# First modulation quarter summed by k-tile, with two weight units loaded and split in parts

## Chip, cores, metric

One core of one Trainium2 chip. The metric is device time in microseconds (us) of one execution, taken as the median of several runs. TensorE (PE) multiplies, VectorE (DVE), ScalarE (ACT) and GpSimd (POOL) work on elements, SyncE (SP) issues most DMAs.

## What is computed

One layer of a transformer block on 512 tokens of width 1024, all in float32. What matters here is its beginning:

```python
mod = jax.nn.silu(c) @ ada_w[layer] + ada_b[layer]            # c: [1, 1024], ada_w: [1024, 6144]
shift1, scale1, gate1, shift2, scale2, gate2 = jnp.split(mod[:, None, :], 6, axis=-1)
h = rmsnorm(x, norm1_w[layer]) * (1 + scale1) + shift1        # [512, 1024]
gq, gk, gv, gr, g_lr, aq, ak, av, merge_a, merge_b = jnp.split(h @ w_in[layer], split_at, axis=-1)
```

Gated linear attention, dilated attention, the merging and a convolutional feed-forward layer follow; the change doesn't touch them.

## The kernel before

The width of 1024 is cut in 8 k-tiles of 128. To keep float32 accuracy with a fast matrix format, each operand of a product is split into a high part (ScalarE converts) and a low part (VectorE subtracts the high part), and three products are made: high by high, low by high, high by low. Weights come in units of 1 MB (`raw`, two slots), which ScalarE turns into `w_hi` and VectorE into `w_lo`. `hi_done` counts units with a high part, `raw_used` units with a low part; the second also frees the slot of `raw` for the DMA that waits for it in `load(q)`.

The first three units are the value weights: unit 0 (`v`, 256 columns of all 8 k-tiles), units 1 and 2 (`vw`, 512 columns of k-tiles 0 to 3 and 4 to 7). They are multiplied while the normalised input is still being made, quarter by quarter; quarter j is k-tiles 2j and 2j + 1. For each quarter:

- The modulation. `ada_w`'s columns for shift and scale of the two k-tiles land in two halves of 1 MB (`load_first(j)`, line 437; half 0 are rows of k 0 to 3, half 1 rows of k 4 to 7). VectorE multiplies each of 8 rows of 128 x 512 by a column of `c_silu` and adds them up in place (`ada_sums(j, half)`, lines 1111 and 1114; quarter 1 leaves one row to TensorE). TensorE sums over the partitions with four products against `ones` (`shift_scale(j)`, line 1732). VectorE adds the bias and makes the gain (`shift_and_gain(j)`, lines 1124 and 1127).
- The input. TensorE transposes a tile of tokens (`normed_tile(k)`, line 1716) into one of four banks, ScalarE copies it out (`normed_out(k)`, line 714, which counts `xn_sb`), makes the high part of the modulated tile once the gain is there (`high(k)`, line 684) and then the tile itself (`modulated(k)`, line 689); VectorE makes the low part (`lower(k)`, line 1137).
- The products. `quarter_hi(j)` is `first_hi` of two k-tiles (unit 0, line 1990) and then `wide_hi` of two (units 1 and 2, line 2020), high input against high and low weights; `quarter_lo(j)` is `first_lo` (line 1998) and `wide_lo` (line 2025), low input against high weights. `wide_hi(0)` writes the four banks that the transposes use, so it waits for `xn_sb` 5 to 8.

Each engine runs its instructions in the order in which the code lists them, and waits at the head for semaphores. Before the change TensorE's list is: six transposed tiles, `shift_scale(0)`, two tiles, `quarter_hi(0)`, `shift_scale(1)`, `quarter_lo(0)`, `quarter_hi(1)`, `shift_scale(2)` and so on. VectorE's: `ada_sums(0, 0)`, `ada_sums(0, 1)`, `shift_and_gain(0)`, `split_lo(0)`, `split_lo(1)`, `ada_sums(1, 0)`, `ada_sums(1, 1)`, `lower(0)`, `lower(1)`, `shift_and_gain(1)`, ... ScalarE's: four `normed_out`, `split_hi(0)`, `high(0)`, `high(1)`, `split_hi(1)`, four `normed_out`, `modulated(0)`, `modulated(1)`, `high(2)`, ... SP's: `load_first(0)`, `load(0)`, `load(1)`, `load_first(1)`, `load_first(2)`, `load(2)`, `load_first(3)`, `load(3)`, then the spill of `xn`.

Of the kernel before, what the change touches and what calls it, by code (L numbers as in the profile page):

```python
# [16 lines left out]
P = 128  # L17
# [146 lines left out]
DIRECT = {1: KT - 1}  # L164
ADA_STEPS = [KT - (j in DIRECT) for j in range(KT // 2)]
SPLIT_K = 5


def hybrid_block_kernel(nc, x, c, positions, ada_w, ada_b, norm1_w, w_in, gate_w2, gate_b, gla_norm_w,
# [3 lines left out]
    with ctx:  # L173
# [132 lines left out]
        spilled, x_back = sem("spilled"), [sem(f"x_back{i}") for i in range(2)]  # L306
        ada_step, ident_in = sem("ada_step"), sem("ident_in")
        mod1_ps, mod_done, gain_done = sem("mod1_ps"), sem("mod_done"), sem("gain_done")
        sq_done, sum_done, ssq_ps, ln_done, rstd_done = (sem(n) for n in (
# [52 lines left out]
        def normed(k):  # L362

            return n_first[:, k, :] if k < LATE else cs[:, k - LATE, :]

        def last_tile(n):
# [55 lines left out]
        def _(sp):  # L422
# [61 lines left out]
            def shuffle(j):  # L484
# [5 lines left out]
                for half in range(2):  # L490
                    for a in range(4):
                        sp.dma_start(qk[32 * half:32 * half + 32, g, a // 2, a % 2, :],  # L492
                                     rope[32 * a:32 * a + 32, j % 2, half, :]).then_inc(qk_in[j % 2], 16)

            load_first(0)
            load(0)
            load(1)
            load_first(1)
# [132 lines left out]
        def _(act):  # L631
# [48 lines left out]
            def high(k):  # L680

                act.wait_ge(gain_done, k // 2 + 1)
                act.wait_ge(xn_sb, k + 1)
                act.activation(h_hi[:, k, :], xn[:, k, :], ACT.Identity, scale=gain[:, 0, k:k + 1],
                               bias=mod[:, k:k + 1]).then_inc(hh_done, 1)
# [25 lines left out]
            def normed_out(k):  # L711

                act.wait_ge(xn_ps, k + 1)
                act.activation(xn[:, k, :], bank[3 + k % 4][:, :], ACT.Copy).then_inc(xn_sb, 1)

            scaled_tokens(0)
            scaled_tokens(1)
            for k in range(4):
                normed_out(k)
            split_hi(0)  # L720
            high(0)
            high(1)
            split_hi(1)
            for k in range(4, KT):
                normed_out(k)
            modulated(0)
            modulated(1)
            for k in (2, 3):
# [366 lines left out]
        def _(dve):  # L1095
# [8 lines left out]
            def ada_sums(j, half):  # L1104
# [4 lines left out]
                for k in range(half * KT // 2, (half + 1) * KT // 2):  # L1109
                    if k == 0:  # L1110
                        dve.tensor_scalar(total, total, c_silu[:, 0:1], None, ALU.mult).then_inc(ada_step, 1)
                    elif k != DIRECT.get(j):
                        dve.wait_ge(ada_step, sum(ADA_STEPS[:j]) + k)
                        dve.scalar_tensor_tensor(total, ada_rows(j, k), c_silu[:, k:k + 1], total,
                                                 ALU.mult, ALU.add).then_inc(ada_step, 1)

            mod_v = mod[:, 0:2 * KT].rearrange("p (s k) -> p s k", s=2)
            bias_v = vecs[:, V_AB:V_AB + 2 * KT].rearrange("p (s k) -> p s k", s=2)

            def shift_and_gain(j):  # L1120
                two = slice(2 * j, 2 * j + 2)
                dve.wait_ge(mod1_ps, j + 1)
                dve.wait_ge(vec_sb, 1)
                dve.tensor_tensor(mod_v[:, :, two], bank[7][:, 4 * j:4 * j + 4].rearrange("p (s k) -> p s k", s=2),
                                  bias_v[:, :, two], ALU.add).then_inc(mod_done, 1)
                dve.wait_ge(mod_done, j + 1)
                dve.scalar_tensor_tensor(gain[:, 0, two], mod_v[:, 1, two], 1.0, vecs[:, V_N1 + 2 * j:V_N1 + 2 * j + 2],
                                         ALU.add, ALU.mult).then_inc(gain_done, 1)

            def lower(k):  # L1130
# [302 lines left out]
            for b in range(1, NB):  # L1433
                sum_squares(b)
            ada_sums(0, 0)
            ada_sums(0, 1)
            shift_and_gain(0)
            split_lo(0)
            split_lo(1)
            ada_sums(1, 0)  # L1440
            ada_sums(1, 1)
            lower(0)
            lower(1)
            shift_and_gain(1)
            ada_sums(2, 0)
# [248 lines left out]
        def _(pe):  # L1694
# [12 lines left out]
            pe.transpose(bank[2][:, 0:ROWS_A], rows_a[:, :], ident[0:ROWS_A, 0:ROWS_A]).then_inc(vec_ps, 1)  # L1707

            def normed_tile(k):

                if k >= 4:
                    pe.wait_ge(xn_sb, k - 3)
                for b in range(NB):
                    if k == 0:
                        pe.wait_ge(xs_done, b + 1)
                    last = pe.transpose(bank[3 + k % 4][:, b * P:(b + 1) * P], x_tok[:, b, k * P:(k + 1) * P], ident)
                last.then_inc(xn_ps, 1)

            def shift_scale(j):

                for rows, moving, first in ((DIRECT.get(j), c_silu, True), (0, ones, False)):
# [9 lines left out]
                    for n in range(4):  # L1731
                        last = pe.matmul(bank[7][:, 4 * j + n:4 * j + n + 1], ada_rows(j, rows)[:, n * P:(n + 1) * P],
                                         moving[:, rows:rows + 1], start=(n == 0 and (first or j not in DIRECT)),
                                         stop=not first, skip_group_check=True)
                last.then_inc(mod1_ps, 1)

            def take(i):
# [244 lines left out]
            def first_hi(k):  # L1982

                if k == 0:
                    pe.wait_ge(raw_used, 1)
                pe.wait_ge(hh_done, k + 1)
                for blk in range(NB):
                    dst = bank[blk // 2][:, blk % 2 * UW:(blk % 2 + 1) * UW]
                    for v in (w_hi, w_lo):
                        pe.matmul(dst, h_hi[:, k, blk * P:(blk + 1) * P], v[:, 0, k * UW:(k + 1) * UW],  # L1990
# [18 lines left out]
            def wide_hi(k):  # L2009

                unit = UNIT[("vw", k // (KT // 2), 0)]
                for part, v in enumerate(wide_weights(k)):
                    if part == 0:
                        pe.wait_ge(hi_done, unit + 1)
# [31 lines left out]

            for k in range(6):
                normed_tile(k)
            shift_scale(0)
            for k in (6, 7):  # L2050
                normed_tile(k)
            quarter_hi(0)
            shift_scale(1)
# [209 lines left out]
```

## Time and profile before

| | |
|---|---|
| median of 3 runs | 927.73 us (926.24 to 928.46) |
| the profiled execution | 928.56 us, span 926.8 us |
| TensorE busy | 899.6 us, 97% of the span |
| TensorE weight loads | 767.6 us, 83% |
| VectorE busy | 493.3 us, 53% |
| ScalarE busy | 369.0 us, 40% |
| GpSimd busy | 36.1 us, 4% |
| chain that ended last | TensorE 88%, SP's queue 3%, ScalarE 3%, VectorE 3%, DMA 2% |

Busy times overlap; an engine that idles while another sets the pace costs nothing. The stretch in question is the first 45 us, in which TensorE still waits for others. "PEclk" is TensorE's granted clock, where 1.00 is 2.4 GHz and 0.50 is 1.2 GHz.

### The profile page before, as it was taken

To read this page: it belongs to the slowest core of one execution; us is meant where nothing else is said; L and a number is where in the kernel's file an instruction comes from. 1 tells how busy PE (TensorE), PEld (TensorE's weight loads), DVE (VectorE), ACT (ScalarE), POOL (GpSimd) and SP (SyncE) were. 2 spreads that over 40 slices of the span, in tenths; PEclk is the share of its full clock that TensorE was granted. 3 is DMA by queue.
4 is the path that set the end of the run, shared out by engine and by line. 5 is a ranking of instruction groups with operands and counts; after the bars stand their busy time and mean duration, and the time that the engine had idled before them with its cause. 6 is when DMAs were issued, how large, how long until landed. Compare 5 with 4: busy or idle time off the path is not lost.

```text
span 926.8 us, 11681 instructions
## 1 busy us (share of the span) xinstructions
PE 899.6 (97%) x4581; PEld 767.6 (83%) x4581; DVE 493.3 (53%) x568; ACT 369.0 (40%) x459; POOL 36.1 (4%) x33
## 2 busy tenths in 40 slices
PE   3999999999999999999999999999999999999996
PEld 3998788989898888887888888888888888888885
DVE  5877875637372737451444667555555555522223
ACT  6442216593533446252223334333333334322235
POOL 0010000000000000000022110000000000000003
PEclk9899999999999999999999999999999999999998
DMA  9965726214351434353233341333333332232202
GB/s 324 347 186 155 195 41 195 65 46 159 114 182 46 160 113 140 133 184 110 71 136 118 112 134 46 92 91 91 91 107 110 99 91 91 105 113 100 91 0 92
DMA packets 117101, 112.91 MB, mean 122 GB/s; under 512 B 7380, under 2 KB 107094, under 8 KB 114631
## 3 DMA queue, kind: packets, MB, share of 16 engines
q1 hardware_dynamic: 116343, 110.21, 38.0%
q10 hardware_dynamic: 720, 2.16, 0.7%
q8 instruction: 27, 0.44, 0.2%
q14 instruction: 11, 0.09, 0.0%
HBM read 104.80 MB, written 4.21 MB: 118 GB/s over the span
## 4 chain that ended last, share of the span: by engine, by line
PE 88%; SPq 3%; ACT 3%; DVE 3%; DMA 2%; issue 1%; DVEq 0%; ACTq 0%
PE bank L1700 25%; PE bank L1702 24%; PE bank L1701 24%; SPq L492 2%; PE bank L2020 1%; DMA raw<-in_w_in_dram 1%; PE bank L2174 1%; PE bank L1921 1%; PE bank L1820 1%; PE bank L1949 1%; DVE w_lo L1154 1%; PE bank L1916 1%; PE bank L2025 1%; PE bank L1815 1%; PE bank L1792 1%
## 5 line engine op out<-in xcount | busy, mean ns | idle before, releaser
L1700 PE MATMUL bank<-h_hi,w_hi 128*128 128x512 f32 x672 | 265.1, 395 | 1.6 <-DVE w_lo L1154 0.8
L1702 PE MATMUL bank<-h_hi,w_lo 128*128 128x512 f32 x672 | 261.7, 389 | 0.0
L1701 PE MATMUL bank<-h_lo,w_hi 128*128 128x512 f32 x672 | 261.6, 389 | 0.0
L1700 PEld LDWEIGHTS bank<-h_hi,w_hi 128*128 128x128 f32 x672 | 126.2, 188 | 28.2 <-issue 2.8
L1702 PEld LDWEIGHTS bank<-h_hi,w_lo 128*128 128x128 f32 x672 | 126.1, 188 | 26.4
L1701 PEld LDWEIGHTS bank<-h_lo,w_hi 128*128 128x128 f32 x672 | 126.3, 188 | 25.3 <-issue 0.2
L1154 DVE TENSOR_TENSOR w_lo<-raw,w_hi 128x2048 fp32r<-128x2048 f32 (+2 forms) x46 | 85.6, 1872 | 86.9 <-ACT w_hi L646 86.9
L1161 DVE TENSOR_TENSOR w_lo<-raw,w_hi 128x2048 fp32r<-128x2048 f32 x31 | 71.1, 2293 | 86.3 <-ACT w_hi L654 86.3
L1654 DVE SCALAR_TENSOR_TENSOR conv<-bank,vecs,conv 128x511 f32<-128x511 f32 x88 | 65.7, 748 | 65.8 <-ACT conv L1046 60.3
L646 ACT ACTIVATE w_hi<-raw 128x2048 fp32r<-128x2048 f32 (+2 forms) x44 | 71.7, 1642 | 50.2 <-DMA raw<-in_w_in_dram 50.1
L654 ACT ACTIVATE w_hi<-raw 128x2048 fp32r<-128x2048 f32 x31 | 59.1, 1906 | 69.3 <-PE bank L1702 69.3
L1046 ACT ACTIVATE conv<-bank,vecs 128x512 f32<-128x512 f32 x44 | 34.2, 779 | 104.7 <-PE bank L1702 104.7
L1700 PE MATMUL bank<-hs_hi,w_hi 128*128 128x512 f32 x176 | 68.6, 390 | 0.0
L1702 PE MATMUL bank<-hs_hi,w_lo 128*128 128x512 f32 x176 | 68.5, 389 | 0.0
L1701 PE MATMUL bank<-hs_lo,w_hi 128*128 128x512 f32 x176 | 68.5, 389 | 0.0
L1700 PEld LDWEIGHTS bank<-hs_hi,w_hi 128*128 128x128 f32 x176 | 33.0, 188 | 6.9
L1702 PEld LDWEIGHTS bank<-hs_hi,w_lo 128*128 128x128 f32 x176 | 33.0, 188 | 6.8
L1701 PEld LDWEIGHTS bank<-hs_lo,w_hi 128*128 128x128 f32 x176 | 33.0, 188 | 6.8
L1700 PE MATMUL bank<-w_hi,h_hi 128*128 128x256 f32 x128 | 37.2, 290 | 0.1
L1701 PE MATMUL bank<-w_lo,h_hi 128*128 128x256 f32 x128 | 36.7, 287 | 0.0
L1702 PE MATMUL bank<-w_hi,h_lo 128*128 128x256 f32 x128 | 36.7, 287 | 0.0
L1188 DVE SCALAR_TENSOR_TENSOR ada_acc<-raw,c_silu,ada_acc 128x2048 f32<-128x2048 f32 x14 | 32.8, 2346 | 0.0
(270 smaller groups left out, 1251.0 us busy)
## 6 DMA issues: line engine op xcount, KB each, us to landing
raw<-in_w_up_dram SPq DMA_DIRECT2D x44, 512.0 KB, 4.9
raw<-in_w_in_dram SPq DMA_DIRECT2D x19, 1024.0 KB, 5.2
raw<-in_ada_w_dram SPq DMA_DIRECT2D x16, 1024.0 KB, 5.4
raw<-in_w_down_dram SPq DMA_DIRECT2D x22, 512.0 KB, 3.6
raw<-in_w_in_dram SPq DMA_DIRECT2D x20, 512.0 KB, 5.2
ada_in<-in_ada_w_dram SPq DMA_DIRECT2D x16, 512.0 KB, 9.8
raw<-in_w_gla_branch_dram SPq DMA_DIRECT2D x4, 1024.0 KB, 5.1
raw<-in_w_out_dram SPq DMA_DIRECT2D x4, 1024.0 KB, 5.0
```

The costliest lines, as they stand in the source:

```text
L492: sp.dma_start(qk[32 * half:32 * half + 32, g, a // 2, a % 2, :], rope[32 * a:32 * a + 32, j % 2, half, :]).then_inc(qk_in[j % 2], 16)
L646: last = act.activation(hv, r, ACT.Copy)
L654: act.activation(w_hi[:, slot, :], raw[:, slot, :], ACT.Copy).then_inc(hi_done, 1)
L1046: act.activation(conv[:, s, t, :], bank[2 * (1 - s) + t][:, :], ACT.Identity, scale=vecs[:, bass.ds(i + (V_CW2 + t * FT), 1)], bias=vecs[: ...
L1154: last = dve.tensor_tensor(lv, r, hv.bitcast(F32), ALU.subtract)
L1161: dve.tensor_tensor(w_lo[:, slot, :], raw[:, slot, :], w_hi[:, slot, :].bitcast(F32), ALU.subtract).then_inc(raw_used, 1)
L1188: ins = dve.scalar_tensor_tensor(ada_acc[:, :], src, c_silu[:, k:k + 1], ada_acc[:, :], ALU.mult, ALU.add)
L1654: ins = dve.scalar_tensor_tensor(conv[:, s, t, tap:SEQ], src[:, 0:SEQ - tap], vecs[:, bass.ds(i + (col + t * FT), 1)], conv[:, s, t, tap:S ...
L1700: pe.matmul(out_ap, wh, xh, start=first, stop=False, skip_group_check=True)
L1701: pe.matmul(out_ap, wh, xl, start=False, stop=False, skip_group_check=True)
L1702: return pe.matmul(out_ap, wl, xh, start=False, stop=last, skip_group_check=True)
L1792: last = pe.matmul(dst[:, j:j + 1], ada_acc[:, j * P:(j + 1) * P], ones[:, 0:1], start=(j == 0), stop=True, skip_group_check=True)
```

## The change

For the first quarter alone:

- VectorE sums its 8 rows for k-tile 0 first (`first_sums(0, ...)`, 256 of the 512 columns), then for k-tile 1; TensorE and VectorE make shift and gain of each k-tile by itself (`first_shift_scale`, `first_shift_and_gain`).
- Units 0 and 1 are loaded (`load_early`) and split (`early_hi`, `early_lo`) in two parts: part 0 is k-tiles 0 and 1, part 1 is the rest. The loads go (unit 0, part 0), (1, 0), (0, 1), (1, 1).
- The first four tiles are transposed block of tokens by block of tokens (`first_tiles`).
- `first_hi(k)` multiplies all blocks by the high weights and then all by the low, for every k.
- The lists of TensorE, VectorE and ScalarE are re-ordered. `hi_done` and `raw_used` are counted by part 1; semaphores of their own count part 0.

```diff
-ADA_STEPS = [KT - (j in DIRECT) for j in range(KT // 2)]
+ADA_STEPS = [2 * KT] + [KT - (j in DIRECT) for j in range(1, KT // 2)]
...
+        def early_columns(n, part):
+
+            return (slice(0, 2 * UW * (n + 1)), slice(2 * UW * (n + 1), UE))[part]
...
+            def load_early(n, part):
+
+                ks = KT if n == 0 else KT // 2
+                rows = (slice(0, 2), slice(2, ks))[part]
+                at, width = (COL_AV, UW) if n == 0 else (COL_AV + UW, 2 * UW)
+                dst = raw[:, n, :].rearrange("p (k n) -> p k n", k=ks)
+                sp.dma_start(dst[:, rows, :], w_in_v[:, rows, at:at + width]).then_inc(
+                    first_in[n] if part == 0 else landed[n], 16)
+
             load_first(0)
-            load(0)
-            load(1)
+            for part in range(2):
+                for n in range(2):
+                    load_early(n, part)
             load_first(1)
             load_first(2)
             load(2)
...
             def high(k):
 
-                act.wait_ge(gain_done, k // 2 + 1)
+                if k == 0:
+                    act.wait_ge(first_gain, 1)
+                else:
+                    act.wait_ge(gain_done, k // 2 + 1)
                 act.wait_ge(xn_sb, k + 1)
...
+            def early_hi(n, part):
+
+                act.wait_ge(first_in[n] if part == 0 else landed[n], 16)
+                cols = early_columns(n, part)
+                last = act.activation(w_hi[:, n, cols], raw[:, n, cols], ACT.Copy)
+                last.then_inc(first_w_hi if part == 0 else hi_done, 1)
+
             scaled_tokens(0)
             scaled_tokens(1)
-            for k in range(4):
+            for k in range(2):
                 normed_out(k)
-            split_hi(0)
+            early_hi(0, 0)
             high(0)
+            for k in range(2, 4):
+                normed_out(k)
+            early_hi(1, 0)
+            for k in range(4, 6):
+                normed_out(k)
             high(1)
-            split_hi(1)
-            for k in range(4, KT):
+            for k in range(6, KT):
                 normed_out(k)
+            early_hi(0, 1)
             modulated(0)
+            early_hi(1, 1)
             modulated(1)
...
+            def first_sums(kk, rows):
+
+                dve.wait_ge(silu_done, 1)
+                for k in rows:
+                    if k % (KT // 2) == 0:
+                        dve.wait_ge(ada_landed[k // (KT // 2)], 32)
+                    own, total = (ada_rows(0, r).rearrange("p (s k n) -> p k s n", s=2, k=2)[:, kk] for r in (k, 0))
+                    if k == 0:
+                        dve.tensor_scalar(total, own, c_silu[:, 0:1], None, ALU.mult).then_inc(ada_step, 1)
+                    else:
+                        dve.wait_ge(ada_step, kk * KT + k)
+                        dve.scalar_tensor_tensor(total, own, c_silu[:, k:k + 1], total,
+                                                 ALU.mult, ALU.add).then_inc(ada_step, 1)
...
+            def first_shift_and_gain(kk):
+
+                one = slice(kk, kk + 1)
+                dve.wait_ge(first_ps if kk == 0 else mod1_ps, 1)
+                dve.wait_ge(vec_sb, 1)
+                dve.tensor_tensor(mod_v[:, :, one], bank[7][:, 0:4].rearrange("p (s k) -> p s k", s=2)[:, :, one],
+                                  bias_v[:, :, one], ALU.add).then_inc(first_mod if kk == 0 else mod_done, 1)
+                dve.wait_ge(first_mod if kk == 0 else mod_done, 1)
+                dve.scalar_tensor_tensor(gain[:, 0, one], mod_v[:, 1, one], 1.0, vecs[:, V_N1 + kk:V_N1 + kk + 1],
+                                         ALU.add, ALU.mult).then_inc(first_gain if kk == 0 else gain_done, 1)
+
+            def early_lo(n, part):
+
+                dve.wait_ge(first_w_hi if part == 0 else hi_done, n + 1)
+                cols = early_columns(n, part)
+                last = dve.tensor_tensor(w_lo[:, n, cols], raw[:, n, cols], w_hi[:, n, cols].bitcast(F32), ALU.subtract)
+                last.then_inc(first_w_lo if part == 0 else raw_used, 1)
...
-            ada_sums(0, 0)
-            ada_sums(0, 1)
-            shift_and_gain(0)
-            split_lo(0)
-            split_lo(1)
+            first_sums(0, range(KT))
+            first_sums(1, range(2))
+            first_shift_and_gain(0)
+            early_lo(0, 0)
+            first_sums(1, range(2, KT))
+            early_lo(1, 0)
+            first_shift_and_gain(1)
+            early_lo(0, 1)
+            early_lo(1, 1)
             ada_sums(1, 0)
-            ada_sums(1, 1)
             lower(0)
             lower(1)
+            ada_sums(1, 1)
             shift_and_gain(1)
...
+            def first_tiles():
+
+                for b in range(NB):
+                    pe.wait_ge(xs_done, b + 1)
+                    for k in range(4):
+                        last = pe.transpose(bank[3 + k][:, b * P:(b + 1) * P], x_tok[:, b, k * P:(k + 1) * P], ident)
+                        if b == NB - 1:
+                            last.then_inc(xn_ps, 1)
+
...
+            def first_shift_scale(kk):
+
+                pe.wait_ge(ones_set, 1)
+                pe.wait_ge(ada_step, (kk + 1) * KT)
+                if kk > 0:
+                    pe.wait_ge(first_mod, 1)
+                for n in (kk, kk + 2):
+                    last = pe.matmul(bank[7][:, n:n + 1], ada_rows(0, 0)[:, n * P:(n + 1) * P], ones[:, 0:1],
+                                     start=(n == 0), stop=True, skip_group_check=True)
+                last.then_inc(first_ps if kk == 0 else mod1_ps, 1)
...
             def first_hi(k):
 
-                if k == 0:
-                    pe.wait_ge(raw_used, 1)
                 pe.wait_ge(hh_done, k + 1)
-                for blk in range(NB):
-                    dst = bank[blk // 2][:, blk % 2 * UW:(blk % 2 + 1) * UW]
-                    for v in (w_hi, w_lo):
+                for v, early, done, value in ((w_hi, first_w_hi, hi_done, 1), (w_lo, first_w_lo, raw_used, 1)):
+                    pe.wait_ge(early if k < 2 else done, value)
+                    for blk in range(NB):
+                        dst = bank[blk // 2][:, blk % 2 * UW:(blk % 2 + 1) * UW]
                         pe.matmul(dst, h_hi[:, k, blk * P:(blk + 1) * P], v[:, 0, k * UW:(k + 1) * UW],
...
                 for part, v in enumerate(wide_weights(k)):
-                    if part == 0:
+                    if k < 2:
+                        pe.wait_ge((first_w_hi, first_w_lo)[part], 2)
+                    elif part == 0:
                         pe.wait_ge(hi_done, unit + 1)
...
-            for k in range(6):
-                normed_tile(k)
-            shift_scale(0)
-            for k in (6, 7):
-                normed_tile(k)
-            quarter_hi(0)
+            first_tiles()
+            first_shift_scale(0)
+            normed_tile(4)
+            normed_tile(5)
+            first_hi(0)
+            normed_tile(6)
+            first_shift_scale(1)
+            normed_tile(7)
+            wide_hi(0)
+            first_hi(1)
+            wide_hi(1)
             shift_scale(1)
             quarter_lo(0)
             quarter_hi(1)
```

## Rows read from the trace of the kernel before

**Rows 1.** The profile page: the span, and TensorE's busy tenths in 40 slices.

```profile
span 926.8 us, 11681 instructions
...
PE   3999999999999999999999999999999999999996
```

**Rows 2.** Stretches: busy us (instructions) of PE, weight loads, DVE, ACT, POOL; PEclk, DMA share, GB/s.

```profile
0.00:24.00 24.00, 8.47 (x42) 7.18 (x43) 13.27 (x20) 14.97 (x21) 0.41 (x5) 0.99 0.97 325
24.00:34.00 10.00, 9.49 (x52) 9.40 (x53) 8.73 (x13) 4.24 (x7) 0.00 (x0) 0.84 1.09 355
34.00:64.00 30.00, 30.00 (x168) 29.25 (x168) 24.58 (x39) 11.10 (x13) 3.39 (x3) 0.94 0.89 274
64.00:927.00 863.00, 851.61 (x4324) 721.76 (x4323) 446.68 (x499) 338.66 (x419) 32.27 (x25) 0.99 0.35 108
```

**Rows 3.** Timeline, TensorE: start us, us, operation, count, idle before it and releaser.

```profile
15.60 4.74 PE L1716 MATMUL bank<-cst,x_tok 128*128 128x128 f32 x21 [0.57 <-ACT x_tok L709]
...
23.79 0.58 PE L1990 MATMUL bank<-w_hi,h_hi 128*128 128x256 f32 x1 [1.72 <-DVE w_lo L1154]
...
32.58 1.02 PE L1732 MATMUL bank<-ones,ada_in 128*128 128x1 f32 x8 [0.51 <-DVE ada_in L1114]
```

**Rows 4.** Waits of TensorE from 60 us on: us in total, times, longest.

```profile
PE bank L1700 <- DVE w_lo L1154: 0.8, 2, 0.5
```

**Rows 5.** Timeline, VectorE; the row of 16.30 us is of a narrower stretch.

```profile
13.32 0.49 DVE L1111 TENSOR_SCALAR ada_in<-ada_in,c_silu 128x512 f32<-128x512 f32 x1 [1.31 <-DMA ada_in<-in_ada_w_dram]
13.84 5.57 DVE L1114 SCALAR_TENSOR_TENSOR ada_in<-ada_in,c_silu 128x512 f32<-128x512 f32 x7
...
16.30 0.75 DVE L1114 SCALAR_TENSOR_TENSOR ada_in<-ada_in,c_silu 128x512 f32<-128x512 f32 x1
...
21.18 0.16 DVE L1124 TENSOR_TENSOR mod<-bank,vecs 128x4 f32<-128x4 f32 x1 [1.76 <-PE bank L1732]
...
24.92 2.29 DVE L1154 TENSOR_TENSOR w_lo<-raw,w_hi 128x2048 fp32r<-128x2048 f32 x1 [1.18 <-ACT w_hi L646]
27.13 0.48 DVE L1111 TENSOR_SCALAR ada_in<-ada_in,c_silu 128x512 f32<-128x512 f32 x1
27.65 4.79 DVE L1114 SCALAR_TENSOR_TENSOR ada_in<-ada_in,c_silu 128x512 f32<-128x512 f32 x6
...
36.69 1.29 DVE L1137 TENSOR_TENSOR h_lo<-n_first,h_hi 128x512 fp32r<-128x512 f32 x2
37.89 3.11 DVE L1114 SCALAR_TENSOR_TENSOR ada_in<-ada_in,c_silu 128x512 f32<-128x512 f32 x4
```

**Rows 6.** SP's issues, each followed by its time from issue to landing in us.

```profile
4.89 3.26 SPq L437 DMA_DIRECT2D ada_in<-in_ada_w_dram  x1
ada_in<-in_ada_w_dram SPq DMA_DIRECT2D x1, 512.0 KB, 11.3
...
26.72 1.42 SPq L472 DMA_DIRECT2D raw<-in_w_in_dram  x1
DMA to landing us min/median/max: 10.0/10.0/10.0
```

**Rows 7.** VectorE's groups by shape: count | busy us, mean ns | idle before.

```profile
L1154 DVE TENSOR_TENSOR w_lo<-raw,w_hi 128x1024 fp32r<-128x1024 f32 x12 | 14.1, 1220 | 3.0 <-ACT w_hi L646 3.0
L1619 DVE SCALAR_TENSOR_TENSOR ntmp<-x,gain,rstd 128x256 f32<-128x256 f32 x10 | 4.8, 484 | 3.4 <-ACT rstd L1025 2.7
```

**Rows 8.** Timeline, ScalarE.

```profile
21.57 1.52 ACT L684 ACTIVATE h_hi<-xn,mod,gain 128x512 fp32r<-128x512 f32 x2 [0.42 <-DVE gain L1127]
24.80 2.04 ACT L714 ACTIVATE xn<-bank 128x512 f32<-128x512 f32 x4
```

**Rows 9.** ScalarE's group of conversions over 1024 columns.

```profile
L646 ACT ACTIVATE w_hi<-raw 128x1024 fp32r<-128x1024 f32 x12 | 12.0, 1049 | 34.8 <-DMA raw<-in_w_in_dram 34.8
```

**Rows 10.** Stretches of `quarter_lo(0)` and `quarter_lo(1)`, columns as in rows 2.

```profile
33.47:37.91 4.44, 4.44 (x18) 3.94 (x18) 4.30 (x10) 3.87 (x5) 0.00 (x0) 0.62 1.08 361
44.50:47.52 3.02, 3.02 (x18) 2.98 (x18) 2.71 (x6) 2.45 (x4) 0.00 (x0) 1.00 1.05 434
```

More of the change, by code:

```diff
@@ L307, in hybrid_block_kernel @@
         ada_step, ident_in = sem("ada_step"), sem("ident_in")
+        first_in, first_w_hi, first_w_lo = [sem(f"first_in{i}") for i in range(2)], sem("first_w_hi"), sem("first_w_lo")
+        first_ps, first_mod, first_gain = sem("first_ps"), sem("first_mod"), sem("first_gain")
         mod1_ps, mod_done, gain_done = sem("mod1_ps"), sem("mod_done"), sem("gain_done")
@@ L1707, in _ @@
             pe.transpose(bank[2][:, 0:ROWS_A], rows_a[:, :], ident[0:ROWS_A, 0:ROWS_A]).then_inc(vec_ps, 1)
+            def first_tiles():
[5 more added lines that the diff above has]
+                            last.then_inc(xn_ps, 1)
             def normed_tile(k):
-                if k >= 4:
-                    pe.wait_ge(xn_sb, k - 3)
+                pe.wait_ge(xn_sb, k - 3)
                 for b in range(NB):
-                    if k == 0:
-                        pe.wait_ge(xs_done, b + 1)
                     last = pe.transpose(bank[3 + k % 4][:, b * P:(b + 1) * P], x_tok[:, b, k * P:(k + 1) * P], ident)
@@ L1982, in first_hi @@
             def first_hi(k):
-                if k == 0:
-                    pe.wait_ge(raw_used, 1)
                 pe.wait_ge(hh_done, k + 1)
-                for blk in range(NB):
-                    dst = bank[blk // 2][:, blk % 2 * UW:(blk % 2 + 1) * UW]
-                    for v in (w_hi, w_lo):
+                for v, early, done, value in ((w_hi, first_w_hi, hi_done, 1), (w_lo, first_w_lo, raw_used, 1)):
+                    pe.wait_ge(early if k < 2 else done, value)
+                    for blk in range(NB):
+                        dst = bank[blk // 2][:, blk % 2 * UW:(blk % 2 + 1) * UW]
                         pe.matmul(dst, h_hi[:, k, blk * P:(blk + 1) * P], v[:, 0, k * UW:(k + 1) * UW],
```

## The prediction

> **What bounds the kernel now.** I read the page first: the span is 926.8 us and TensorE is busy in nearly all of it, except in the first slice [rows 1]. The stretches then say where TensorE is not busy: 15.5 of the first 24 us, 0.5 us of the next 10, and from 64 us on 11.4 us in 863 that are spread thin [rows 2]. All edits lie before 45 us, so the question is when TensorE can begin its unbroken work, and what breaks it. The waits name two breaks after the transposes: 1.7 us before the first weight product (line 1990), for the low weights, and 0.5 us at line 1732, the small column-sum products of the second quarter, `shift_scale(1)` [rows 3]. From 60 us on the longest wait for VectorE is 0.8 us in total over two waits [rows 4]. So behind `shift_scale(1)` there is almost nothing that could absorb a delay: what moves its start moves the end. It starts at 32.58 us, released by VectorE's last multiply-add [rows 3]. The stage has one limiter, the order of work on VectorE, and the whole sum below is the new time of this one product.
>
> VectorE before: it starts its sums at 13.32 us when weights land; eight operations last until 19.41 us; it waits 1.76 us for TensorE's column sums, does the gain, then splits two weight units, 2.29 us each with a wait of 1.18 us for ScalarE between them, and does the second quarter's seven operations from 27.13 to 32.44 us [rows 5].
>
> **The change, part by part.**
>
> *The sums by k-tile.* Eight operations over 512 columns become sixteen over 256. A multiply-add over 512 takes 0.75 us at a pitch of 0.787 us (4.79 us for six, [rows 5]); over 256 columns the nearest row has 484 ns [rows 7], with the same gap of 0.035 us a pitch of 0.52 us. The opening multiply is 0.49 us for 512; for 256 I take 0.35 us, between half of it and all of it. The first half (k-tile 0) would be done 0.35 + 7 x 0.52 = 4.0 us after 13.32 us, at 17.3 us. But the fourth operation's successor needs the second half of the load: its last DMA is issued at 4.89 us and lands 11.3 us later, at 16.2 us [rows 6], and the fifth operation started at 16.30 us in the kernel before [rows 5]. With small operations VectorE gets there at 15.25 us and waits 1.05 us. So k-tile 0 is summed at 16.3 + 4 x 0.52 = 18.35 us, 1.1 us sooner than before instead of 2.1 us. The whole of both sums costs 2 x 0.35 + 14 x 0.52 = 8.0 us against 6.1 us, +1.9 us of VectorE time.
>
> The Trainium skill speaks against such a cut: "VectorE: DVE Perf Modes", section on the TRN2 errata, says that each instruction from SBUF pays a fixed latency, and that tiles should have 512 elements or more so that it is spread. [...]
>
> *First gain.* Two operations of k-tile 1 run ahead of it, to 19.1 us. TensorE's two products (four records, half of the eight that take 1.02 us) run from 18.4 to 18.9 us beside them. Two small operations, 0.16 us each with their gaps, give the gain at 19.45 us, 2.1 us sooner than before, where the first of the two began at 21.18 us and the gain was there at 21.55 [rows 5]. ScalarE makes the first high tile by 20.3 us (1.52 us for two, [rows 8]). Part (0,0) of the weights, 0.25 MB, is next in the DMA queue behind the load that lands at 16.2 us, and at some 350 GB/s [rows 2] follows it by 0.75 us, so it is there; the other three parts (1.75 MB) are there 5 us later.
>
> *Weights split in parts, on VectorE.* Four subtractions (512, 1024, 1536, 1024 columns) take the place of two over 2048: 1024 columns take 1.22 us [rows 7], 2048 take 2.29 us [rows 5], so a column costs 1.04 ns and an instruction 0.15 us. The two more cost 0.3 us. VectorE goes: low (0,0) from 19.4 to 20.0, six sums to 23.1, low (1,0) to 24.2, second gain to 24.55 us.
>
> *ScalarE's order.* This is the step that decides. `high(1)` waits for the second gain (24.55), and behind it in program order are `normed_out(6)` and `(7)` and then `early_hi(0,1)`, the large part of unit 0. `high(1)` is 0.72 us by its pitch, two `normed_out` 0.95 us (2.04 us for four, start to start a little less, [rows 8]), and the conversion of 1536 columns 1.48 us (1049 ns for 1024, [rows 9], and 1.9 us for 2048): high (0,1) is done at 27.9 us. VectorE stands with its next instruction, low (0,1), from 24.55 to 27.95 us: a new wait of 3.4 us, and everything on VectorE, the second quarter's sums included, is queued behind it. Then 1.67 us for (0,1), 1.14 for (1,1), which ScalarE's `early_hi(1,1)` (about 29.6 us) just allows: 30.8 us.
>
> *The second quarter.* Four operations take 0.52 + 3 x 0.79 = 2.9 us, to 33.7. Then come `lower(0)` and `lower(1)`, which stood behind the second half of the sums and now stand ahead of it: 1.2 us by their starts (36.69 to 37.89, the two take 1.29 us, [rows 5]), to 34.9. Three more operations, 2.4 us: 37.2 us. With the 0.13 us that TensorE took to follow VectorE, `shift_scale(1)` starts at 37.3 us, against 32.58: **+4.7 us**.
>
> *TensorE's order and the weights high before low.* The transposes go block by block: the last four start at 15.6 us, at a pitch of 0.23 us (4.74 us for 21, [rows 3]), so all four tiles stand at 16.7 us. `first_hi(0)` starts near 20.7 us, 3.1 us sooner than 23.79. But `wide_hi(0)` waits for `xn_sb` 7 and 8 behind ScalarE's `high(1)`, until about 26 us; the quarter's products are through at 30 to 32.5 us, depending on the clock. In the kernel before they ended at 31.3. All of it lies in front of 37.3 us, so the rearrangement costs or gains nothing: it is covered by VectorE, with 5 us to spare. The number of products is unchanged.
>
> *DMA order.* Two more issues on SP, with the same bytes; the DMA engines are fully busy until past 34 us in any case [rows 2]. `load(2)` waits for `raw_used` 1, which now comes with low (0,1) at 29.6 us, where it was issued at 26.72 us; four more loads (`load_first(3)`) and `load(3)` are queued behind it on SP. It landed 10.0 us after its issue [rows 6], so at worst at 39.6 us. ScalarE wants it after `shift_scale(1)` and four tiles and more, near 41.5 us: covered by 2 us. If that cover were gone, its low part would move by the excess, and VectorE has 1.5 us of idle there before it would show.
>
> *What follows 37.3 us.* `quarter_lo(0)` runs at once, its low tiles being ready. Before, it took 4.44 us with a mean granted clock of 0.62; the same block of the next quarter took 3.02 us at 1.00 [rows 10]. In the new kernel TensorE has idled for some 5 us before it, and so starts it at 1.2 GHz too. Bounds: 3.02 us if the clock were high (-1.4 us), twice that if it were low all through (+1.6 us). The low stretch before began at its start and lasted nearly all of it; now it may begin sooner, with the small products, and end sooner. I take -0.1 us.
>
> **Sum.** +4.7 - 0.1 = +4.6 us. The profiled execution took 928.56 us (926.8 us of span and 1.8 us around it), 0.8 us above the median of 927.73; its sum is 933.2 us, and by the median 932.3 us. Slower, by 0.5%.
>
> **Rivals.**
> 1. *VectorE's new wait is smaller than I have it.* If no operation of VectorE waited for ScalarE, its own work alone, with the wait for the landing, would put `shift_scale(1)` at 37.3 - 3.4 = 33.9, so +1.3 us: about 929.0 us, too close to tell from no change unless part of the wait stays. For it: ScalarE's order is read from the code, not seen. Against it: every instruction of the chain is in program order, and each has a row. 7%.
> 2. *Not slower, by the clock.* If TensorE, having worked on small pieces since 18 us, kept 2.4 GHz into `quarter_lo(0)`, 1.4 us of [rows 10] would come back. It outweighs the delay only where rival 1 holds as well: +1.3 - 1.4 = -0.1 us, 927.6 us; with an earlier landing of the second load half (up to 1.05 us of waiting gone) 926.6 us. It decides once the stall of 3.4 us is gone. Against it: a wait of 0.5 us with small products around it was followed by the low clock [rows 3, 10], and the new gap is ten times that. 4% for no change, 4% for faster.
> 3. *The low clock costs more.* All of `quarter_lo(0)` at 1.2 GHz: +4.7 + 1.6 = +6.3 us, 934.0 us. The Trainium skill, "TensorE: Matmul & The Clock Gate", section on oscillation in real kernels, tells that every long gap sends the array back to its low clock and makes the next work start cold; by that the long gap is worse than the short one. That the small products come first speaks against the full price. 12%.
> 4. *The change does not do what it says* (the first product no sooner): then the first gain stays at 21.5 us, and the chain behind it, unchanged in length, ends 2 us later, +6.7 us, 934.4 us. 3%.
>
> The forecast itself, with the second quarter waiting for VectorE at 36.3 to 38.3 us: 70%.
>
> **Range and chances.** The forecast's own range is 931 to 933.5 us. The unknowns are the clock (-1.4 to +1.6), the operation lengths (some 0.5 us over the chain) and the scatter of the runs (926.24 to 928.46). I give 929.8 to 934.3, which leaves rivals 1 and 2 outside. About 0.2%, 1.9 us, is what can be told from no change. Slower 0.88 (the forecast, rivals 3 and 4, 3% of rival 1), same 0.08 (4% of rival 1, 4% of rival 2), faster 0.04 (rival 2).
>
> **What would show it.** In the profile after: line 1732's products for the first quarter near 18.4 and 23.1 us; first product of line 1990's kind near 20.7 us; VectorE's fifth small sum starting at 16.3 us; a wait of about 3.4 us of VectorE for ScalarE's `w_hi` ahead of the 1536-column subtraction; TensorE idle for some 5 us up to 37.3 us, released by the multiply-add; and from there the same order as before, 4.6 us later. Wrong would be: TensorE's longest idle before 20 us only, VectorE's 1536-column subtraction starting before 26 us, or a stretch after 64 us in which TensorE idles less than now.

## The result, and the profile after

The changed kernel takes 934.18 us (median of 6 runs, 933.34 to 936.36) against 927.2 us before (6 runs, 926.24 to 928.46): a ratio of 1.0082, 95% interval 1.0071 to 1.0093. It is 7.0 us slower, where +4.6 us and 932.3 us were forecast. The median itself lies just inside the range of 929.8 to 934.3 us; but the forecast stood on a baseline of 927.73 us, and on that the ratio gives 935.3 us, above the range. The sign and the place were right, the size was not. In the profiled executions the spans are 932.8 and 926.8 us, 6.0 us apart.

The page of the changed kernel, with its span, TensorE's busy tenths and its granted clock:

```profile
span 932.8 us, 11709 instructions
...
PE   4799999999999999999999999999999999999996
...
PEclk9799999999999999999999999999999999999998
```

Its stretches (busy us of PE, weight loads, DVE, ACT, POOL; PEclk, DMA share, GB/s):

```profile
0.00:24.00 24.00, 10.99 (x48) 9.22 (x49) 14.39 (x30) 13.56 (x22) 0.41 (x5) 1.00 0.96 325
24.00:37.00 13.00, 7.00 (x37) 6.37 (x36) 9.07 (x12) 5.51 (x7) 0.00 (x0) 0.88 1.09 356
37.00:64.00 27.00, 27.00 (x143) 26.11 (x144) 19.06 (x31) 11.07 (x13) 3.38 (x3) 0.87 0.77 235
```

TensorE is busy 2.5 us more in the first 24 us than in [rows 2], the early start that the change makes, and then idles for 6 of the next 13 us. VectorE shows why (timeline: start us, us, operation, count, idle before it and its releaser):

```profile
12.57 0.35 DVE L1157 TENSOR_SCALAR ada_in<-ada_in,c_silu 128x256 f32<-128x256 f32 x1 [0.93 <-DMA ada_in<-in_ada_w_dram]
...
15.49 2.05 DVE L1160 SCALAR_TENSOR_TENSOR ada_in<-ada_in,c_silu 128x256 f32<-128x256 f32 x4 [1.01 <-DMA ada_in<-in_ada_w_dram]
...
24.01 0.16 DVE L1184 SCALAR_TENSOR_TENSOR gain<-mod,vecs 128x1 f32<-128x1 f32 x1
27.40 2.90 DVE L1191 TENSOR_TENSOR w_lo<-raw,w_hi 128x1536 fp32r<-128x1536 f32 x2 [3.23 <-ACT w_hi L739]
30.21 0.48 DVE L1143 TENSOR_SCALAR ada_in<-ada_in,c_silu 128x512 f32<-128x512 f32 x1
...
32.97 1.29 DVE L1201 TENSOR_TENSOR h_lo<-n_first,h_hi 128x512 fp32r<-128x512 f32 x2
34.17 2.32 DVE L1146 SCALAR_TENSOR_TENSOR ada_in<-ada_in,c_silu 128x512 f32<-128x512 f32 x3
```

These answer to [rows 5]. A wait of 3.23 us for ScalarE stands ahead of the 1536-column subtraction, and the second quarter's sums end at 36.5 us instead of 32.4. ScalarE meanwhile, which answers to [rows 8]:

```profile
24.21 0.81 ACT L703 ACTIVATE h_hi<-xn,mod,gain 128x512 fp32r<-128x512 f32 x1 [1.41 <-DVE gain L1184]
24.93 1.06 ACT L733 ACTIVATE xn<-bank 128x512 f32<-128x512 f32 x2
25.89 1.48 ACT L739 ACTIVATE w_hi<-raw 128x1536 fp32r<-128x1536 f32 x1
```

It waited 1.41 us for VectorE's gain first, then made VectorE wait for what stood behind. TensorE, which answers to [rows 3]:

```profile
20.13 1.20 PE L2074 MATMUL bank<-w_hi,h_hi 128*128 128x256 f32 x4
...
36.64 1.84 PE L1806 MATMUL bank<-ones,ada_in 128*128 128x1 f32 x8 [5.30 <-DVE ada_in L1146]
38.33 2.06 PE L2082 MATMUL bank<-w_hi,h_lo 128*128 128x256 f32 x8
40.19 3.62 PE L2111 MATMUL bank<-w_hi,h_lo 128*128 128x512 f32 x8
43.60 0.86 PE L2074 MATMUL bank<-w_hi,h_hi 128*128 128x256 f32 x4
```

The first product of weights comes at 20.13 us, 3.7 us sooner than before (2.9 us when both are counted from VectorE's first sum), and all of that lead is spent at line 1806 (line 1732 before), with 5.30 us of idle. The stretch of `quarter_lo(0)`, which answers to [rows 10], is at 1.2 GHz from end to end:

```profile
38.33:43.60 5.27, 5.27 (x17) 4.55 (x18) 4.91 (x10) 4.70 (x5) 0.00 (x0) 0.50 1.14 323
```

TensorE's waits from 64 us on, which answer to [rows 4], have one that was not there, for ScalarE's exponentials (the second row):

```profile
PE bank L1768 <- DVE w_lo L1218: 1.0, 2, 0.7
...
PE bank L1916 <- ACT S L789: 0.4, 1, 0.4
```

### The profile page after: what moved, and what is told of

Same layout as the page of the kernel before. It is cut to its first block, busy times and chain, and to the rows that moved or that the text cites. A ratio compares the mean times of both kernels' runs of the same rounds, so it can differ in the third digit from the quotient of the medians.

```text
span 932.8 us, 11709 instructions
## 1 busy us (share of the span) xinstructions
PE 902.5 (97%) x4581; PEld 769.7 (83%) x4581; DVE 494.7 (53%) x580; ACT 368.7 (40%) x461; POOL 36.0 (4%) x33
## 4 chain that ended last, share of the span: by engine, by line
PE 87%; DVE 3%; SPq 3%; DMA 3%; ACT 2%; issue 1%; DVEq 0%; ACTq 0%
PE bank L1768 25%; PE bank L1769 24%; PE bank L1770 24%; SPq L498 1%; DMA raw<-in_w_in_dram 1%; PE bank L2106 1%; PE bank L2265 1%; DMA ada_in<-in_ada_w_dram 1%; PE bank L2006 1%; PE bank L2111 1%; PE bank L1905 1%; PE bank L2034 1%; DVE w_lo L1218 1%; PE bank L2001 1%; PE bank L1900 1%
## 5 line engine op out<-in xcount | busy, mean ns | idle before, releaser
L1218 DVE TENSOR_TENSOR w_lo<-raw,w_hi 128x2048 fp32r<-128x2048 f32 (+2 forms) x44 | 81.0, 1853 | 86.6 <-ACT w_hi L662 86.4
L662 ACT ACTIVATE w_hi<-raw 128x2048 fp32r<-128x2048 f32 (+2 forms) x42 | 67.9, 1630 | 50.4 <-DMA raw<-in_w_in_dram 50.3
```

The source lines that it names most:

```text
L662: last = act.activation(hv, r, ACT.Copy)
L1218: last = dve.tensor_tensor(lv, r, hv.bitcast(F32), ALU.subtract)
```

## The experiments

Two theories are to be told apart. **Order:** VectorE's list (the wait for ScalarE, `lower` ahead of the sums, the small sums) sets `shift_scale(1)`, and with it the end. **Clock:** TensorE's granted clock after the gap makes the rest. A rival to both is that the split of the first quarter itself costs the 7 us. The landing of the first load moves all times by up to 0.9 us from one execution to the next (VectorE's first sum starts at 12.38 to 13.32 us in the profiles), so below `shift_scale(1)` is counted from VectorE's first sum; before, that is 32.58 - 13.32 = 19.26 us, after 36.64 - 12.57 = 24.07 us.

### before_again: the kernel before, unchanged

> The kernel before, unchanged, for a second profile. The low-clock theory (the length of TensorE's half-speed stretch over quarter_lo(0) differs from execution to execution, and with it the time) expects a stretch of another length than 3.8 us and a time that differs from 926.8 us of span by half of the difference, up to 1.5 us. The rival (the 6.0 us between the two profiles are all order of work) expects the same stretch and a span within 0.3 us once the landing times are taken off. Ratio 1.000 to within 0.002 by both.

Measured: 927.22 us (10 runs), ratio 1.0000 (0.9986 to 1.0014); its span is 924.2 us.

```profile
13.09 0.49 DVE L1111 TENSOR_SCALAR ada_in<-ada_in,c_silu 128x512 f32<-128x512 f32 x1 [1.11 <-DMA ada_in<-in_ada_w_dram]
...
32.49 1.02 PE L1732 MATMUL bank<-ones,ada_in 128*128 128x1 f32 x8 [0.48 <-DVE ada_in L1114]
...
33.38:37.82 4.44, 4.44 (x18) 3.85 (x18) 4.29 (x10) 3.87 (x5) 0.00 (x0) 0.62 1.07 366
```

The order is the same (19.40 us), and so is the low stretch, against what the clock theory expected here: 4.44 us in both. The 2.6 us by which the spans differ arise behind 64 us. A part of them shows in the clock of one stretch, first of the first profile of before, then of this one:

```profile
264.00:284.00 20.00, 20.00 (x155) 19.34 (x154) 10.05 (x14) 6.70 (x7) 0.00 (x0) 0.91 0.37 107
```

```profile
264.00:284.00 20.00, 20.00 (x158) 18.87 (x157) 11.60 (x14) 6.11 (x7) 0.00 (x0) 1.00 0.37 106
```

20 us at a mean of 0.91 hold some 3.5 us at half speed, in one execution and not in the other. The price can be read off: from the block of small products ahead of it (line 1921, at 270.30 us) to the next such block it took 49.85 us, in this run 48.30, so 1.5 us. So a single pair of profiles compares to 2 us or so, no better.

### after_again: the changed kernel, unchanged

> The changed kernel, unchanged, for a second profile. Expected: the same order of all operations with the second half of the first weights landing within 0.7 us of 15.4 to 16.2 us, shift_scale(1) 4.6 us after where the kernel before has it, and quarter_lo(0) again wholly at 1.2 GHz. From shift_scale(1) to the first product of quarter_hi(1) it took 6.96 us in the first profile; the low-clock theory expects 6.2 to 7.0. Time 934 us.

Measured: 934.51 us (4 runs), ratio 1.0081 (1.0065 to 1.0097), span 931.8 us.

```profile
13.10 0.35 DVE L1157 TENSOR_SCALAR ada_in<-ada_in,c_silu 128x256 f32<-128x256 f32 x1 [1.17 <-DMA ada_in<-in_ada_w_dram]
...
37.21 1.84 PE L1806 MATMUL bank<-ones,ada_in 128*128 128x1 f32 x8 [4.68 <-DVE ada_in L1146]
...
43.16 0.64 PE L2074 MATMUL bank<-w_hi,h_hi 128*128 128x256 f32 x4
```

37.21 - 13.10 = 24.11 us: the order gives the same figure to 0.04 us, 4.8 us more than the mean of the two profiles before. But from line 1806 to `quarter_hi(1)` it took 5.95 us instead of 6.96 (5.33 us before), a little below what was expected: the low clock ended sooner, so `quarter_lo(0)` was not wholly at 1.2 GHz here. The order is the same in both, the price of the clock is not.

### lower_back: the two lower() behind the sums again

```diff
             ada_sums(1, 0)
+            ada_sums(1, 1)
             lower(0)
             lower(1)
-            ada_sums(1, 1)
             shift_and_gain(1)
```

> The changed kernel with lower(0) and lower(1) put back behind the second half of the second quarter's sums. The VectorE-order theory expects shift_scale(1) 1.2 us sooner (35.4 instead of 36.6 us), and the end 1.2 us sooner, about 933.0 us. The rival, that VectorE's order doesn't set the time, expects no difference.

Measured: 932.24 us, ratio 1.0046 (1.0028 to 1.0064). VectorE's first sum is at 13.02 us, so line 1806 comes after 23.13 us, 0.96 us sooner than the 24.09 of the two profiles after:

```profile
36.15 1.84 PE L1806 MATMUL bank<-ones,ada_in 128*128 128x1 f32 x8 [3.72 <-DVE ada_in L1146]
```

The order theory holds; 1.2 us were expected for this, and why it is 0.2 us less was not tried. The median is 1.9 to 2.3 us below the two of the changed kernel, more than the order alone gives; from line 1806 to `quarter_hi(1)` this profile took 6.37 us, between the 6.96 and 5.95 of the changed kernel.

### hi_early: ScalarE's large part ahead of high(1)

```diff
+            early_hi(0, 1)
             high(1)
             for k in range(6, KT):
                 normed_out(k)
-            early_hi(0, 1)
             modulated(0)
```

> The changed kernel with ScalarE's early_hi(0,1) ahead of high(1) instead of behind it and two tiles copied out. The VectorE-order theory expects VectorE's wait of 3.2 us ahead of the 1536-column subtraction to fall to near 0; a second wait of some 1.8 us then appears ahead of low (1,1), because early_hi(1,1) still comes late: shift_scale(1) 1.4 us sooner, the end 1.4 us sooner, about 932.8 us. If the wait for ScalarE were harmless, no difference; if ScalarE's order for TensorE mattered more (wide_hi(0) waits for tiles 6 and 7), the time would rise by up to 0.3 us.

Measured: 930.94 us (8 runs), ratio 1.0039 (1.0025 to 1.0054).

```profile
24.62 1.76 DVE L1191 TENSOR_TENSOR w_lo<-raw,w_hi 128x1536 fp32r<-128x1536 f32 x1
28.06 1.23 DVE L1191 TENSOR_TENSOR w_lo<-raw,w_hi 128x1024 fp32r<-128x1024 f32 x1 [1.68 <-ACT w_hi L739]
...
35.63 1.83 PE L1806 MATMUL bank<-ones,ada_in 128*128 128x1 f32 x8 [3.92 <-DVE ada_in L1146]
```

The wait of 3.2 us is gone and one of 1.68 us stands a step later. Counted from the first sum at 12.98 us, line 1806 comes after 22.65 us, 1.44 us sooner, as expected. The medians say more than that, 3.2 to 3.6 us. In its profile neither a half-speed spell behind 200 us (1.5 us) nor the wait for the exponentials occurs. These lie far behind the edit's own place; why they should be rarer here was not tried.

### sums_first: the second quarter's sums ahead of the large low parts

```diff
-            early_lo(0, 1)
-            early_lo(1, 1)
             ada_sums(1, 0)
+            ada_sums(1, 1)
+            early_lo(0, 1)
+            early_lo(1, 1)
             lower(0)
             lower(1)
-            ada_sums(1, 1)
             shift_and_gain(1)
```

> The changed kernel with VectorE's list re-ordered: the second quarter's seven sums right after the second gain, then low (0,1) and (1,1), then lower(0) and lower(1). The VectorE-order theory expects the sums to end near 29.5 us, before TensorE is through with quarter_hi(0) (31.3 us), so that shift_scale(1) follows without a wait: 5.3 us sooner than in the changed kernel, or 1.3 us sooner than in the kernel before. Then quarter_lo(0) may wait for lower(1) (33.7 us or so) by up to 1.5 us. With the clock kept high 927 us less 1 to 2, 925.5 us; with the low stretch 927 us. The rival, that the first quarter's split by k-tile itself costs the 7 us, expects 934 us as before.

Measured: 926.2 us (10 runs), ratio 0.9989 (0.9977 to 1.0000).

```profile
25.27 4.79 DVE L1146 SCALAR_TENSOR_TENSOR ada_in<-ada_in,c_silu 128x512 f32<-128x512 f32 x6
...
32.13 1.03 PE L1806 MATMUL bank<-ones,ada_in 128*128 128x1 f32 x8
33.52 1.40 PE L2082 MATMUL bank<-w_hi,h_lo 128*128 128x256 f32 x8 [0.36 <-DVE h_lo L1201]
```

The sums end at 30.0 us, while TensorE is still in `quarter_hi(0)`; line 1806 follows with no wait, 5.0 us sooner than in the changed kernel (19.12 us from the first sum). The whole loss of the change is gone, with every part of it still in place but the order of five lines. The stretch of low clock isn't gone: `quarter_lo(0)` took 4.62 us, near the 4.44 of the kernel before. That settles the rival: the split into k-tiles and parts does not cost 7 us by itself; the order on VectorE does, with the low clock that follows from its long gap.

### after_fill: superfluous transposes in the gap

```diff
                     else:
+                        if j == 1:
+                            for _ in range(36):
+                                pe.transpose(bank[2][:, 3 * P:4 * P], x_tok[:, 0, 0:P], ident)
                         pe.wait_ge(ones_set, 1)
                         pe.wait_ge(ada_step, sum(ADA_STEPS[:j + 1]))
```

> The changed kernel with 36 superfluous transposes on TensorE between the two halves of shift_scale(1), where it idles for 5.3 us; at 0.13 us each they last 4.6 us and end before VectorE releases the products. The low-clock theory expects the granted clock to stay 1.00 through quarter_lo(0), which then takes about 3.0 us, so from shift_scale(1) to quarter_hi(1) 4.0 us instead of 6.96: the end 2.3 to 3 us sooner than the changed kernel, 931.5 us. The rival, that the late start alone (VectorE's order) makes up the whole loss and the clock only scatters it, expects no gain, 934 us.

Measured: 929.0 us (10 runs), ratio 1.0021 (1.0009 to 1.0033).

```profile
33.30 4.13 PE L1805 MATMUL bank<-cst,x_tok 128*128 128x128 f32 x36
37.27 0.97 PE L1809 MATMUL bank<-ones,ada_in 128*128 128x1 f32 x8
...
41.13 0.64 PE L2077 MATMUL bank<-w_hi,h_hi 128*128 128x256 f32 x4
...
38.10:41.13 3.03, 3.03 (x19) 2.99 (x18) 2.71 (x6) 2.46 (x4) 0.00 (x0) 1.00 1.10 346
```

Line 1806's place (1809 here) is unchanged, 24.09 us after the first sum, so VectorE's order is untouched, and yet the kernel is 5 us faster. The clock theory holds: the products take 0.97 instead of 1.84 us, `quarter_lo(0)` 3.03 us instead of 5.27 and 4.25, together 3.86 us instead of 6.96 and 5.95. By the profiles that is 2.1 to 3.1 us; the medians give 5.2 to 5.5. The profile can't show the other 2 to 3 us: its execution took 930.78 us, 1.8 us above the median, with a half-speed spell at 324 us in it. The mean granted clock of the single executions says where to look. Five of these ten have 0.997 and took 927.6 to 929.0 us, the other five, the profiled one among them, 0.994 or 0.995; of the ten executions of the changed kernel none is above 0.992. So the rest goes with less time at half speed elsewhere; why the filled gap should bring that isn't shown.

### before_fill: the same in the kernel before, five transposes

> The kernel before with 5 superfluous transposes (0.65 us) in the same place, where TensorE idles for 0.5 us. If the low clock follows the idle 0.5 us, it stays high, quarter_lo(0) takes 3.0 us and not 4.4, and the end comes 1.3 us sooner, 925.9 us. If it follows the 1.8 us of one-column products (which remain), nothing changes, 927.2 us.

Measured: 926.32 us (10 runs), ratio 0.9992 (0.9982 to 1.0001).

```profile
31.64 0.74 PE L1731 MATMUL bank<-cst,x_tok 128*128 128x128 f32 x5
32.24 1.02 PE L1735 MATMUL bank<-ones,ada_in 128*128 128x1 f32 x8
...
33.13:36.15 3.02, 3.02 (x18) 2.98 (x18) 2.87 (x7) 2.45 (x4) 0.00 (x0) 1.00 1.09 374
```

In the profile 0.65 us of useless work in a gap of 0.5 us keeps the clock at 1.00, and `quarter_lo(0)` takes 3.02 instead of 4.44 us. The transposes outlast the gap and push line 1732 (1735 here) back to 19.71 us after the first sum, where it stood at 19.26 and 19.40, so up to `quarter_hi(1)` some 1.0 us is left of the 1.4. The medians gain 0.8 us, which the interval doesn't part from nothing; so the effect is shown for the stretch and not for the time. It isn't that one execution's luck: 7 of these 10 have a mean granted clock of 0.995 or more, of 27 of the kernel before measured beside them one has.

### lower_first, lower_only, tile_six: is there more

lower_first puts `lower(0)` and `lower(1)` right behind the sums of sums_first (the first part below is against that run, the second against the changed kernel) and makes `shift_scale(1)`'s first four products ahead of `wide_hi(1)`; `shift_scale` itself, which takes the two halves as an argument, is not shown:

```diff
             ada_sums(1, 0)
             ada_sums(1, 1)
+            lower(0)
+            lower(1)
             early_lo(0, 1)
             early_lo(1, 1)
-            lower(0)
-            lower(1)
             shift_and_gain(1)
...
             wide_hi(0)
             first_hi(1)
+            shift_scale(1, (True,))
             wide_hi(1)
-            shift_scale(1)
+            shift_scale(1, (False,))
```

> The changed kernel with VectorE's second-quarter sums and lower(0), lower(1) ahead of low (0,1) and (1,1), and shift_scale(1)'s first four products moved ahead of wide_hi(1). Both waits of TensorE in this stretch should be gone: quarter_lo(0) starts at 33.1 us without the 0.4 us for lower(1). The order theory expects 0.4 us less than the version with the sums first, 925.8 us; if one-column products standing together also lower the clock, parting them keeps it high and saves up to 1.5 us more, 924.5 us. A rival, that the later low (0,1), and with it load(2), now holds up quarter_hi(1) or the third unit, expects 927 us or more.

Measured: 925.53 us (10 runs), ratio 0.9982 (0.9971 to 0.9992): 1.6 us faster than the kernel before. The rival, 927 us or more by the later load, is out; against 926.2 us for sums_first the gain is not clear of noise.

```profile
28.19 0.95 PE L1806 MATMUL bank<-c_silu,ada_in 128*128 128x1 f32 x8
...
31.09 0.95 PE L1806 MATMUL bank<-ones,ada_in 128*128 128x1 f32 x8
...
31.89:34.92 3.03, 3.03 (x19) 2.99 (x19) 2.96 (x6) 1.15 (x2) 0.00 (x0) 1.00 0.49 122
```

`quarter_lo(0)` starts with no wait and at full clock. lower_only has VectorE's list of lower_first, with the products left together:

> The changed kernel with VectorE's list re-ordered as in the best version so far (second quarter's sums, then lower(0) and lower(1), then low (0,1) and (1,1)), but with the eight one-column products of shift_scale(1) left standing together. No wait of TensorE is left here, so this parts two causes of the low clock. If standing one-column products (1.8 us) bring the low clock on by themselves, quarter_lo(0) takes 4 us or more at a granted clock below 0.8 and the time is that of the version with the sums first, 926.2 us. If a wait is needed beside them, the clock stays at 1.00, quarter_lo(0) takes 3.0 us and the time is 925.5 us, as with the products parted.

Measured: 925.45 us (11 runs), ratio 0.9987 (0.9976 to 0.9997), and 16 records of one-column products in a row with the clock at 1.00 behind them:

```profile
32.20 0.95 PE L1806 MATMUL bank<-c_silu,ada_in 128*128 128x1 f32 x8
33.01 1.03 PE L1806 MATMUL bank<-ones,ada_in 128*128 128x1 f32 x8
...
33.90:36.92 3.02, 3.02 (x18) 2.98 (x18) 2.78 (x7) 2.45 (x4) 0.00 (x0) 1.00 0.98 302
```

So the one-column products don't lower the clock by themselves in this execution; a wait next to them (0.5 us before, 0.36 us in sums_first) goes with it. The case is less clean than was expected, as TensorE ran at half speed just before, in `quarter_hi(0)`:

```profile
28.00:30.00 2.00, 2.00 (x9) 1.81 (x9) 1.93 (x4) 2.00 (x3) 0.00 (x0) 0.50 1.10 347
```

It had waited 0.94 us for tiles 6 and 7 at 25.9 us. The same wait of 0.68 us (tile_six) and 0.85 us (lower_first) was followed by no such stretch, that of 1.00 us in after_fill was. So a short wait can bring the low clock and need not; what decides it was not found.

tile_six moves `normed_out(6)` ahead of `high(1)` in lower_first:

> The best version so far (sums and lower first, products parted) with ScalarE's normed_out(6) moved ahead of high(1). With VectorE's delay gone, TensorE's own wait of 0.85 us inside wide_hi(0) for tiles 6 and 7 is on the path; it should shrink to some 0.2 us, and the end comes 0.5 us sooner, 925.0 us. If VectorE still sets the time there (its sums end at 29.4 us), no difference, 925.5 us.

Measured: 925.21 us (12 runs), ratio 0.9982 (0.9970 to 0.9994). TensorE's wait in `wide_hi(0)` only fell from 0.85 to 0.68 us, where 0.2 was expected, since tile 7 is still behind `high(1)`. Not to be told from lower_first.

## Why the prediction was off

- *Where it is decided.* Right. All edits were weighed by the start of `shift_scale(1)`; forecast 37.3 us with the first sum at 13.32, that is 23.98 us after it, measured 24.07 and 24.11. The forecast +4.7 us is +4.8 and +4.7 by the two pairs of profiles.
- *The small sums.* Right: 0.35 us and a pitch of 0.51 us; the wait of 1.05 us for the second half of the load is 1.01 us.
- *First gain.* The two products of a k-tile (four records) were taken as half of 1.02 us; they take 0.99. Counted from the first sum, both gains come some 0.4 us later than forecast; terms behind them that were a little too long take up all but 0.1 us of it at line 1806.
- *ScalarE's order.* Right: 3.4 us forecast, 3.23 us measured. The forecast's own terms, 24.55 + 0.72 + 0.95 + 1.48, give 27.7 us, not the 27.9 that it went on with. hi_early removes it and moves line 1806 by what was reckoned.
- *lower ahead of the sums.* 1.2 us forecast, 0.96 us by lower_back.
- *TensorE's order, the loads.* Covered, as said: TensorE reached line 1806 with 5.3 us to spare, and the third unit's late load shows in no wait of this stretch.
- *What follows.* **This step failed.** The forecast gave the low clock -0.1 us, arguing that the small products would take up the start of the low stretch. Two things were wrong in it. The one-column products were priced as if the clock didn't touch them; at 1.2 GHz they take 1.84 us instead of 1.02. And in three of four profiles they did not shorten what the low clock takes of `quarter_lo(0)`: it took 5.27, 4.25, 4.68 and 4.56 us in after, after_again, lower_back and hi_early, against 4.44 before. The clock fell in the gap itself, at about 33.9 us in after and 35.1 us in after_again, and rose at 44.1 and 41.9 us. From line 1806 to `quarter_hi(1)` that is 6.96, 5.95, 6.37 and 6.26 us, against 5.33: +0.6 to +1.6 us where -0.1 stood. Rival 3, with 12%, had the right direction, and its +6.3 us is near the measured +7.0, but by luck: it put all of +1.6 us on `quarter_lo(0)` at 1.2 GHz, taken as twice 3.02 us. Wholly at a granted clock of 0.50 it took 5.27 us, 1.75 times 3.02 and 0.8 us more than before; the other 0.8 us in that execution are the small products, which rival 3 did not price either. In all four profiles the work behind the gap of 3.7 to 5.3 us starts at a granted clock of 0.50. The Trainium skill, "TensorE: Matmul & The Clock Gate", section on oscillation in real kernels, says that a long gap makes the next work start cold, and these traces agree.
- *The rest.* The forecast held that behind `shift_scale(1)` everything moves by the same amount. The new wait for exponentials (0.4 and 0.5 us in after and after_again, 0 in both profiles before) and a half-speed spell of 1.5 us, which is in both profiles of the changed kernel and in one of two before, break that; the forecast had no term for either. Counted from VectorE's first sum to the end, the first pair of profiles differs by 6.75 us: 4.8 for the order, 1.6 for the clock and 0.4 for the wait make 6.8, with the spell in both. The second pair differs by 7.6 us: 4.7, 0.6, 0.5, and 1.5 for the spell that only the changed kernel has there, make 7.3. So the two pairs are accounted for to 0.3 us, and the 7.0 us of the medians lies between them. Of what was missed, some 1.2 us are the failed step (+1.1 as the mean of the two profiles of the changed kernel, where -0.1 stood). That the spell is more frequent in the changed kernel would fit, but with two profiles of each it is argued, not shown, and what brings the wait for the exponentials was not tried: it is in seven of the nine profiles with the change's split, the fast ones of lower_first, lower_only and tile_six among them, and not in sums_first and hi_early.
- *The range.* Its upper end took rival 3's price only as the edge and left nothing for the scatter on top of it.

## What to carry to other kernels

When work is split so that a consumer can start sooner, look at what then stands between the first consumer and the next one in every engine's list: here TensorE's first product came 2.9 us sooner and the next quarter's column sums 4.8 us later, because on VectorE they stood behind a wait for ScalarE and behind work that nobody needed yet. Moving five lines made 934 us into 926. And a gap that grows on TensorE has two prices, the gap and the low clock behind it; in the four profiles with a gap of 3.7 to 5.3 us the work behind it started at half speed each time, so such a gap should be charged with it, small products included.

## What the runs showed of the hardware

- One-column float32 products with a full weight load slow down with the clock like wide ones: 8 records in 1.84 us at a granted clock of 0.50, 0.95 us at 1.00.
- 36 transposes that nobody reads, in a gap of TensorE, kept the granted clock at 1.00 behind it and made a kernel 5 us faster (after_again 934.51, after_fill 929.0 us).
- The work of `quarter_lo(0)` takes 3.02 us at a granted clock of 1.00 and 5.27 us at 0.50, 1.75 times as long and not twice.
- The same kernel's executions spread over 6 us (923.8 to 929.8 us in 23 runs), though the first 64 us of two profiles agree to 0.1 us. The clock is only a part of it: in before_again an execution at a mean granted clock of 0.995 took 928.25 us and one at 0.993 took 925.64.
- A spell of some 3.5 us at half speed is in six of the twelve profiles, once in each, with no wait of TensorE from 200 to 345 us in any of the six. In all six it begins within 1 us of the end of one of four blocks of 16 products of 32 columns (line 1921 in the kernel before, 1.92 us in most), at 224 to 327 us. The other 42 such blocks are followed by none, so the block alone isn't the cause.
